# Expert weights of a mixture-of-experts decoder step in pieces of 1 MB instead of 512 KB

## The reference, cut to what matters

```
def expert_block(args):
    e, tok = args
    xb = x_pad[tok]                                     # 128 x 1024
    hmid = jax.nn.silu(xb @ w_gate[e]) * (xb @ w_up[e]) # 1024 x 512 each
    return hmid @ w_down[e]                             # 512 x 1024
```

## Time and profile before

| | |
|---|---|
| median of three runs | 1613.69 us |
| profiled execution, its own time | 1615.27 us |
| its span | 1613.2 us |
| busy: PE, DVE, ACT, POOL | 90%, 71%, 50%, 35% |
| HBM read, written | 315.93 MB, 59.64 MB |
| queue q1 (loads and stores by descriptors of the hardware) | 321.51 MB |
| queue q0 (POOL's) | 37.87 MB |
| first weight load of the experts issued | 943.79 us |
| last matmul of the experts | about 1555 us |

### The profile page before, as it was taken

The page is one execution under the profiler, slowest core; times in us unless marked ns, Lnnn a source line. Parts: engine busy times, 40 slices in busy tenths (PEclk is TensorE's granted clock), DMA queues, the critical chain, the costliest instruction groups (busy, mean ns, idle before and its releaser), DMA issues. The chain is left out here.

```text
span 1613.2 us, 22828 instructions
## 1 busy us (share of the span) xinstructions
PE 1448.9 (90%) x7691; PEld 1254.3 (78%) x7691; DVE 1150.6 (71%) x1505; ACT 800.5 (50%) x1086; POOL 558.7 (35%) x365
## 2 busy tenths in 40 slices
PE   4999999989999999899999529999999999999940
PEld 3899999989999998788776427788888888887830
DVE  4488722267676675446665567999999999999937
ACT  5232222223343333344353327777877877777713
POOL 5423323534444442383644001633223322221101
PEclk9899999979999999899999659999999999999975
DMA  4122232234343345766553148999999999999857
GB/s 170 41 80 93 94 120 88 90 104 141 129 143 128 128 143 165 268 185 231 179 167 121 59 184 320 396 383 390 381 369 378 383 371 376 372 373 376 303 212 298
DMA packets 165604, 360.25 MB, mean 223 GB/s; under 512 B 20740, under 2 KB 50372, under 8 KB 164484
## 3 DMA queue, kind: packets, MB, share of 16 engines
q1 hardware_dynamic: 149972, 321.51, 56.0%
q0 software_dynamic: 15568, 37.87, 7.0%
HBM read 315.93 MB, written 59.64 MB: 233 GB/s over the span
## 5 line engine op out<-in xcount | busy, mean ns | idle before, releaser
L61 PE MATMUL bank<-xh,wh 128*128 128x352 f32 x864 | 290.0, 336 | 3.5 <-ACT raw L829 2.9
L63 PE MATMUL bank<-xh,wl 128*128 128x352 f32 x864 | 282.4, 327 | 0.0
L62 PE MATMUL bank<-xl,wh 128*128 128x352 f32 x864 | 281.9, 326 | 0.0
L1772 ACT CAST wg_h<-wg 128x1024 fp32r<-128x1024 f32 x128 | 135.6, 1059 | 110.5 <-DMA wu<-in_w_up 56.3
L1684 POOL DMA_INDIRECT scratch_picked<-yb,dst x32 | 89.9, 2811 | 249.4 <-DVE yb L1875 249.4
L61 PEld LDWEIGHTS bank<-xh,wh 128*128 128x128 f32 x864 | 166.0, 192 | 13.0 <-issue 10.8
L1881 DVE TENSOR_TENSOR wg_l<-wg,wg_h 128x1024 fp32r<-128x1024 f32 x128 | 156.7, 1224 | 24.7 <-ACT wu_h L1773 23.4
L62 PEld LDWEIGHTS bank<-xl,wh 128*128 128x128 f32 x864 | 166.3, 192 | 2.6 <-issue 1.9
L1524 POOL TENSOR_TENSOR wol<-wo,woh 128x1024 fp32r<-128x1024 f32 x48 | 118.2, 2475 | 141.2 <-ACT woh L907 141.0
L63 PEld LDWEIGHTS bank<-xh,wl 128*128 128x128 f32 x864 | 166.1, 192 | 0.0
L1882 DVE TENSOR_TENSOR wu_l<-wu,wu_h 128x1024 fp32r<-128x1024 f32 x128 | 156.4, 1222 | 0.0
(11 more groups left out here) (345 smaller groups left out, 3369.6 us busy)
## 6 DMA issues: line engine op xcount, KB each, us to landing
wg<-in_w_gate SPq DMA_DIRECT2D x128, 512.0 KB
wu<-in_w_up SPq DMA_DIRECT2D x128, 512.0 KB
wd<-in_w_down SPq DMA_DIRECT2D x128, 512.0 KB
wo<-in_w_out SPq DMA_DIRECT2D x48, 512.0 KB, 4.2
w<-in_w_in_tiles SPq DMA_DIRECT2D x36, 512.0 KB, 3.8
yy<-scratch_picked SPq DMA_DIRECT2D x8, 1024.0 KB, 13.0
scratch_xb<-stage POOLq DMA_DIRECT2D x10, 512.0 KB, 4.0
xb<-scratch_xb SPq DMA_DIRECT2D x8, 640.0 KB, 3.9
```

Of the source, the lines that this page charges most:

```text
L61: nc.tensor.matmul(acc, lh, rh, start=start, stop=False)
L62: nc.tensor.matmul(acc, lh, rl, start=False, stop=False)
L63: return nc.tensor.matmul(acc, ll, rh, start=False, stop=stop)
L1772: nc.scalar.copy(wg_h[:, s, :], wg[:, s, :])
```

## The change

Pieces are twice as large. Two loads of 1 MB per matrix take the place of four of 512 KB, and ACT's casts and DVE's subtracts have 2048 elements per partition instead of 1024. There are two instead of four steps of each semaphore. ACT and DVE do one of the two gate/up pieces ahead of silu and hid, and one behind, where they did three ahead and one behind. PE waits at k = 0 and 4 instead of 0, 2, 4 and 6, and at f = 0 and 2.

```
-                at = [held(sp, i * 4 + (p - 3)) for p in range(4)]
-                for p in range(4):
+                at = [held(sp, i * 2 + (p - 1)) for p in range(2)]
+                for p in range(2):
                     wait(sp, gu_split, at[p])
-                    rows = slice(2 * p * P, (2 * p + 2) * P)
+                    rows = slice(4 * p * P, (4 * p + 4) * P)
                     for t, name in ((wg, "w_gate"), (wu, "w_up")):
-                        sp.dma_start(t[:, 2 * p:2 * p + 2, :], ...
+                        sp.dma_start(t[:, 4 * p:4 * p + 4, :], ...
...
-                    sp.dma_start(wd[:, p, :], ...
+                    sp.dma_start(wd[:, 2 * p:2 * p + 2, :], ...
...
-                    if k % 2 == 0:
-                        pe.wait_ge(gu_split, i * 4 + (k // 2 + 1))
+                    if k % 4 == 0:
+                        pe.wait_ge(gu_split, i * 2 + (k // 4 + 1))
...
-                    if k % 2:
+                    if k % 4 == 3:
                         last.then_inc(gu_used, 1)
...
-                    last.then_inc(down_used, 1)
+                    if f % 2:
+                        last.then_inc(down_used, 1)
...
-                    wait(act, gu_used, i * 4 + (p - 3))
-                    s = slice(2 * p, 2 * p + 2)
+                    wait(act, gu_used, i * 2 + (p - 1))
+                    s = slice(4 * p, 4 * p + 4)
                     nc.scalar.copy(wg_h[:, s, :], wg[:, s, :])
                     nc.scalar.copy(wu_h[:, s, :], wu[:, s, :]).then_inc(gu_high, 1)
...
-                    nc.scalar.copy(wd_h[:, p, :], wd[:, p, :]).then_inc(down_high, 1)
+                    nc.scalar.copy(wd_h[:, 2 * p:2 * p + 2, :], wd[:, 2 * p:2 * p + 2, :]).then_inc(down_high, 1)
...
-                high_gate_up(i + 1, range(3))
+                high_gate_up(i + 1, range(1))
                 silu(i)
                 high_x(i + 1)
-                high_gate_up(i + 1, range(3, 4))
+                high_gate_up(i + 1, range(1, 2))
                 high_down(i)
                 high_hid(i)
...
-                low_gate_up(i + 1, range(3))
+                low_gate_up(i + 1, range(1))
                 gated(i)
                 low_x(i + 1)
-                low_gate_up(i + 1, range(3, 4))
+                low_gate_up(i + 1, range(1, 2))
                 low_down(i)
```

More of the change, by code:

```diff
@@ L1604, in experts @@
         zeroed, rows_psum, rows_ready = sem("zeroed"), sem("rows_psum"), sem("rows_ready")
-        gate_up_loaded = [sem(f"gate_up_loaded{p}") for p in range(4)]
-        down_loaded = [sem(f"down_loaded{p}") for p in range(4)]
+        gate_up_loaded = [sem(f"gate_up_loaded{p}") for p in range(2)]
+        down_loaded = [sem(f"down_loaded{p}") for p in range(2)]
         src_ready, dst_ready, xg_loaded = sem("src_ready"), sem("dst_ready"), sem("xg_loaded")
@@ L1631, in load_gate_up @@
                 e = expert(i)
-                at = [held(sp, i * 4 + (p - 3)) for p in range(4)]
-                for p in range(4):
+                at = [held(sp, i * 2 + (p - 1)) for p in range(2)]
+                for p in range(2):
                     wait(sp, gu_split, at[p])
-                    rows = slice(2 * p * P, (2 * p + 2) * P)
+                    rows = slice(4 * p * P, (4 * p + 4) * P)
                     for t, name in ((wg, "w_gate"), (wu, "w_up")):
-                        sp.dma_start(t[:, 2 * p:2 * p + 2, :], A[name][e, rows, :].rearrange("e (k p) f -> p (e k) f", p=P)).then_inc(gate_up_loaded[p], 16)
+                        sp.dma_start(t[:, 4 * p:4 * p + 4, :], A[name][e, rows, :].rearrange("e (k p) f -> p (e k) f", p=P)).then_inc(gate_up_loaded[p], 16)
             def load_down(i):
                 e = expert(i)
-                at = [held(sp, i * 4 + (p - 3)) for p in range(4)]
-                for p in range(4):
+                at = [held(sp, i * 2 + (p - 1)) for p in range(2)]
+                for p in range(2):
                     wait(sp, down_split, at[p])
-                    sp.dma_start(wd[:, p, :], A["w_down"][e, p * P:(p + 1) * P, :].rearrange("e p d -> p (e d)")).then_inc(down_loaded[p], 16)
+                    sp.dma_start(wd[:, 2 * p:2 * p + 2, :], A["w_down"][e, 2 * p * P:(2 * p + 2) * P, :].rearrange("e (k p) d -> p (e k) d", p=P)).then_inc(down_loaded[p], 16)
             m = blocks_but_three(sp) + 1
@@ L1730, in down @@
                 for f in range(FF // P):
-                    pe.wait_ge(down_split, i * 4 + (f + 1))
+                    if f % 2 == 0:
+                        pe.wait_ge(down_split, i * 2 + (f // 2 + 1))
                     for n in range(2):
@@ L1775, in high_down @@
             def high_down(i):
-                for p in range(4):
+                for p in range(2):
                     act.wait_ge(down_loaded[p], i * 16 + 16)
-                    wait(act, down_used, i * 4 + (p - 3))
-                    nc.scalar.copy(wd_h[:, p, :], wd[:, p, :]).then_inc(down_high, 1)
+                    wait(act, down_used, i * 2 + (p - 1))
+                    nc.scalar.copy(wd_h[:, 2 * p:2 * p + 2, :], wd[:, 2 * p:2 * p + 2, :]).then_inc(down_high, 1)
             def high_x(i):
@@ L1783, in high_x @@
                     act.wait_ge(xT_psum, i * 2 + (half + 1))
-                    wait(act, gu_used, i * 4)
+                    wait(act, gu_used, i * 2)
                     nc.scalar.copy(xh[:, 4 * half:4 * half + 4, :], bank[4 + half][:].rearrange("p (k t) -> p k t", k=4)).then_inc(x_high, 1)
             def silu(i):
-                act.wait_ge(gu_used, i * 4 + 4)
+                act.wait_ge(gu_used, i * 2 + 2)
                 wait(act, hid_ready, i)
@@ L1794, in high_hid @@
                 act.wait_ge(hT_psum, i + 1)
-                wait(act, down_used, i * 4)
+                wait(act, down_used, i * 2)
                 nc.scalar.copy(hT_h[:], bank[6][:].rearrange("p (k t) -> p k t", k=4)).then_inc(h_high, 1)
             m = blocks_but_three(act) + 1
-            high_gate_up(0, range(4))
+            high_gate_up(0, range(2))
             high_x(0)
             def block_of(i):
-                high_gate_up(i + 1, range(3))
+                high_gate_up(i + 1, range(1))
                 silu(i)
                 high_x(i + 1)
-                high_gate_up(i + 1, range(3, 4))
+                high_gate_up(i + 1, range(1, 2))
                 high_down(i)
@@ L1872, in unload_y @@
                 wait(dve, y_stored, i * 16)
-                dve.wait_ge(down_used, i * 4 + 4)
+                dve.wait_ge(down_used, i * 2 + 2)
                 for n in range(2):
@@ L1878, in low_gate_up @@
                 for p in pieces:
-                    dve.wait_ge(gu_high, i * 4 + (p + 1))
-                    s = slice(2 * p, 2 * p + 2)
+                    dve.wait_ge(gu_high, i * 2 + (p + 1))
+                    s = slice(4 * p, 4 * p + 4)
                     nc.vector.tensor_tensor(wg_l[:, s, :], wg[:, s, :], wg_h[:, s, :].bitcast(F32), ALU.subtract)
@@ L1891, in low_down @@
             def low_down(i):
-                for p in range(4):
-                    dve.wait_ge(down_high, i * 4 + (p + 1))
-                    nc.vector.tensor_tensor(wd_l[:, p, :], wd[:, p, :], wd_h[:, p, :].bitcast(F32), ALU.subtract).then_inc(down_split, 1)
+                for p in range(2):
+                    dve.wait_ge(down_high, i * 2 + (p + 1))
+                    ks = slice(2 * p, 2 * p + 2)
+                    nc.vector.tensor_tensor(wd_l[:, ks, :], wd[:, ks, :], wd_h[:, ks, :].bitcast(F32), ALU.subtract).then_inc(down_split, 1)
             def low_hid(i):
@@ L1901, in _ @@
             m = blocks_but_three(dve) + 1
-            low_gate_up(0, range(4))
+            low_gate_up(0, range(2))
             low_x(0)
             def block_of(i, first=False):
-                low_gate_up(i + 1, range(3))
+                low_gate_up(i + 1, range(1))
                 gated(i)
                 low_x(i + 1)
-                low_gate_up(i + 1, range(3, 4))
+                low_gate_up(i + 1, range(1, 2))
                 low_down(i)
```

## The result

The kernel after takes 1641.51 us (median of 4 runs, 1636.14 to 1644.74), the kernel before beside it 1614.18 (4 runs). The ratio is 1.0165, 95% interval 1.0145 to 1.0186: about 27 us slower, where 9 were forecast, and outside the range. The profiled execution is the fastest of the four (1636.14, span 1634.1, so 20.9 over the span of before). So the profile shows the loss smaller than it mostly is: the medians carry some 6 us more.

The account below looks back on a forecast made before the run. DMA was taken as the slower of two nearly equal bounds, beside PE. Ramp 7.3, landing to PE 1.3, tail 2.0 and fewer DMAs -1.5 summed to +9.1 us, median 1622.5; range 1608 to 1637 (forecast's own 1617 to 1629).

Parts of the forecast that it names:

- casts and subtracts of 2048: ACT's casts and DVE's subtracts of weight pieces: one doubled instruction takes 1.98 and 2.30 us.
- ramp, block 2's first load: Start of the expert stage: block 2's first load waits for block 1's first split, 6.8 to 7.8 us later, taken as 7.3.
- landing to gate_up: From the first gate/up half's landing to PE's gate_up: 9.9 us for cast, subtract and hid, +1.3 us once.
- tail: End of the last block: the larger last wd subtract delays copies of y and the last down, +2.0 us.
- fewer DMAs: Weight loads, 6 instead of 12 DMAs a block: fewer boundaries in the full queue save 1.5 us.
- turn of one buffer: One gate/up raw buffer from load issue to next issue: 9.7 + 5.4 + 1.1 = 16.2 us, under the block's 18.3.
- new wait: Rival, chance 0.18: DMA runs dry between large loads in every block, 0.5 us a block, 14 us more, total 1637.
- silu at 18.8 with DMA share under 0.98: Sign in the expert blocks: silu spaced by 18.8 us or more with that DMA share would show a new wait.
- larger-transfers rival: Rival, chance 0.14: larger weight DMAs move faster, PE bounds the stage at 17.71 us a block, total 1607.6 us.

Follow-up runs that it names:

- e3: Kernel before with down in two pieces as in the kernel after, gate and up still in four: 1616.27 us, ratio 1.0014.
- e11: Kernel before with each gate/up piece loaded by DMAs of 256 KB, two for one; releases, casts and subtracts as before: 1614.14 us, ratio 1.0002.
- e1: Kernel after with its large casts, subtracts and releases, but each piece loaded by DMAs of 512 KB: 1629.80 us, ratio 1.0099.
- e6: Kernel after without DVE's wg_l subtract (PE takes wg_h twice), so gate/up pieces are released 2.2 us sooner: 1623.87 us, ratio 1.0054.
- e9: Kernel after with DMAs of 512 KB and without DVE's wg_l subtract (release 2.2 us sooner): 1621.42 us, ratio 1.0053.
- e8: Kernel before reading two neighbouring gate/up rows per partition (4 KB packets), x turned with that stride to match: 1614.53 us, ratio 0.9997.
- e12: Kernel before with two neighbouring gate/up rows per partition (4 KB packets) and the copies of y moved from DVE to ACT: 1608.23 us, ratio 0.9962.
- e5: Kernel after with each DVE subtract of 2048 elements made by two of 1024: 1642.55 us, ratio 1.0181.
- e10: Kernel before without DVE's wg_l subtract (PE takes wg_h twice), so pieces are released 1.1 us sooner: 1613.61 us, ratio 1.0001.

## Why the prediction was wrong

The table sets the terms against the profile (20.9 us) and the runs.

| step | predicted | measured |
|---|---|---|
| casts and subtracts of 2048 | 1.98, 2.30 us | 1.91, 2.29 |
| ramp, block 2's first load | 6.8 to 7.8, taken as 7.3 | 9.8, of which the windows up to 1052 keep 7.4 |
| landing to gate_up | 9.9 us (+1.3) | 9.8 (cast 1517.45, 0.1 behind the landing; matmul 1527.17) |
| tail | +2.0 | +2.1 behind the last silu; e3 in all 2.3 |
| fewer DMAs | -1.5 | 0 in a full queue (e11), +10.6 in after |
| turn of one buffer | 16.2, under 18.3 | 18.5, the bound |

**The step that failed** is the slack of the "new wait", held to be positive in the mean at 16.2 against 18.3. Its constant part was right (8.6 against 8.5). The load's part, 7.6 us from issue to landing, was that of an empty queue whose 16 engines finish together; it measured 10.0 and 9.4. So the rival with 0.18 came true as a mechanism. Its price of 14 us on top of the forecast stands against 10.6 that the loop costs (after beside e1). That its total, 1637, comes near the 1641.5 is partly luck: the other 7 us of the 17.5 above the forecast (26.6 by the ratio, against 9.1) lie outside the loop, with the -1.5, the ramp and the tail among them. Its own mark for telling it, silu at 18.8 with DMA share under 0.98, did not come out: the trace has 18.54 and 0.99 to 1.00. The stream slows long before the share shows it.

**The terms that were mis-sized.** The ramp lacked POOL's gather: the copy was followed through DVE's long instructions, the indirect DMA behind it was not. And -1.5 was set from a best slice of the page, which is no evidence that boundaries cost anything. With ramp 9.3 (e1's first load of block 2 stands 29.0 us behind POOL's first copy, before 19.7), 1.3 and a tail of 2.7, e1 would be at +13.3; its profile has 13.9 in span, or 14.4 counted from that copy, and its runs 16.0. Some 3 us between these 13.3 and the runs' 16.0 stay open. The remaining 10.6 of after is the loop.

**The larger-transfers rival** (0.14) has fallen. The Trainium skill, "DMA: Bandwidth & Descriptors", section "Bandwidth", asks for 1 MiB or more per DMA; in this kernel 256 KB makes no difference against 512 KB (e11 beside before), nor 1 MB where the release is soon enough (e6 beside e9), and 1 MB is worse where the release is late (after beside e1).

**Open.** Why a half in two DMAs of 1 MB each for gate and up lands 0.3 to 0.5 us later than in four of 512 KB, and with more scatter, was not found. Both have a dip of the rate behind each late issue. That the 10.0 us are the slowest engine's is read from the marks, and no run changed the engines' balance.

## What to carry to other kernels

For every single-buffered tile write the whole turn (issue, landing by the slowest engine, cast, subtract, release) and compare it with the period. A larger piece lengthens the turn on all its sides at once, and it costs nothing until the slack is used up. Take issue to landing from rows where the queue is short, not from bytes over the best rate. Where an engine shares a way with POOL, follow each POOL instruction up to the load that it releases, and before removing a bound, look at which stalls were free only because of it (e8 and e12).

## What of the hardware was not expected

- POOL waits for DVE's running two-input subtract, for a copy of 128x1 (1.02 us behind instructions of 1024, 2.09 behind 2048) and for an indirect DMA (1.12 and 2.17); e5 puts both back to 1.02 and 1.11. In before three indirect DMAs took 7.4 us each between 1013.6 and 1038.2, while DVE was busy without a gap (24.60 of 24.60 us). With DVE's work reduced (e10, e12) they take 1.0 to 2.5.
- A load's marks come far apart: in before the first of a quarter's 32 comes 3.7 us behind the issue, the 24th at 8.2, the last at 12.1. What a buffer's user waits for is the last (after: last mark at 1517.35, ACT's cast at 1517.45).
- A DMA share of 1.00 went with 370 GB/s in after, and 1.03 with 380 in before.
- With two neighbouring rows of 2 KB read as one packet of 4 KB (e8) the same bytes went through by the 17.8 us of PE's block, with 6.5 to 7.9 us from issue to landing, where with packets of 2 KB a block took 18.3. A packet of 2 KB took 90 ns in before, one of 4 KB 171 in e8.
